# Hymba encoder trunk, first part of the projection: where ScalarE squares the weight chunks and who issues their loads

## Chip, cores and metric

One core of a Trainium2 chip runs the whole program in one launch. The metric is the device time of one execution in microseconds (us), median of several.

## What is computed

The reference is a hybrid encoder trunk of one layer on two groups of tokens (2048 and 256, model width 1024): a Hyena mixer and latent attention side by side, then an expert-choice mixture of experts. Only the start of it matters here, the normalisation and the input projection:

```python
def rms_norm(x, g):
    xf = x.astype(jnp.float32)
    y = xf * lax.rsqrt(jnp.mean(xf * xf, axis=-1, keepdims=True) + EPS)
    return (y * g.astype(jnp.float32)).astype(x.dtype)
...
u = rms_norm(x, attn_norm[l]) @ w_in[l]
y_h = hyena_mixer(u[..., :COL_HYENA], ...)
y_a = mla_mixer(u[..., COL_HYENA:COL_Q], u[..., COL_Q:COL_KV], u[..., COL_KV:], ...)
```

`w_in` has 1536 columns for the Hyena mixer and 416 for the attention.

## The kernel before, in words

The function `project` is the first of the phases, and everything behind it (attention, Hyena, experts) waits for it. It has two parts.

**First part.** A loop over 18 tiles of 128 tokens, one step t per tile, written out by hand on every engine and tied together by semaphores. The tile is normalised, turned (128x128 transposes on PE), split into a high and a low float16 half (`xT`, `xL`), and multiplied by the 416 attention columns (24 matmuls). In the same steps the 1536 Hyena columns, in 12 chunks of 128, are loaded one after another into the single buffer `wch` (512 KB) and squared, so that their common scale is known before the second part. The squares are sums of each chunk; the products are not made here.

In step t each engine does this:

- ScalarE: `square_x(t+2)` (L445), `copy_xT(t+1)` in two halves (L452), `square_chunk(t-2)` for 2 <= t < 14 (L481), `copy_c(t)` (L458, L462, L465), then it issues the load of chunk t-1 into `wch` on its own DMA queue (L517, the helper is L315). The load of chunk 0 is issued at the start (L491); the load that step 13 issues is chunk 0 again, for the second part.
- GpSimd: `root_x(t)` (L400, L402), the reciprocal root of the row's mean square.
- VectorE: `norm(t+2)` (L765), `copy_xT(t+1)`, the low halves (L770), and in some steps the filter angles (`angles` L778, `fold` L790), the scaling of small weights and of the norm gains.
- TensorE: `turn_x(t+1)` (L633), `make_c(t)` (L644), in step 5 also `hidden(1)` (L658).
- Sync engine: for t from 3 on it waits for `norm(t-3)` (the semaphore `normed`) and issues the rows of tile t (`copy_rows`, L170: four DMAs of 128 KB, one of 512 KB for the last two tiles). In its iteration t = 12 it also stores the size `S` (L353, 512 bytes), waits for the second sine (L354) and stores the filter's hidden values `H` (L356, two of 288 KB). Behind the loop it stores `VS` (L358, 512 bytes).

`make_c(t)` waits until `copy_c(t-1)` has emptied the PSUM bank (L639) and for the low halves of tile t (L637). `copy_xT(t+1)` waits for `turn_x(t+1)`; `turn_x(t+1)` waits for `norm(t+1)`.

**Second part.** 60 products of the split chunks with all tokens. Its first product waits for the last `copy_c` (L732) and for the split of chunk 0. The sync engine loads the chunks of this part (L362).

The wait and issue on ScalarE in the code:

```python
def square_chunk(n):
    act.wait_ge(wch_in, 16 * (n + 1))
    if n >= 2:
        act.wait_ge(w_squared["u"], n - 1)
    act.activation(wH[n % 2][:, :, :], wch[:, :, :], ACT.Square, scale=1 / MOST, accum_out=w_sum["u"][:, n:n + 1]
                   ).then_inc(w_squared["u"], 1)
```

Of the kernel before, what the change touches and what calls it, by code (L numbers as in the profile page):

```python
# [127 lines left out]
def rows(t, n=P):  # L128
    return bass.ds(t * n, n)
# [27 lines left out]
def tile_rows(ap, i):  # L157

    g = int(i >= NTP)
    J = P // (GROUPS[g] // N2)  # L160
    return ap.rearrange("(t i j) c -> i j t c", i=N2 // J, j=J)[i - g * NTP]


def copy_rows(eng, tile, ap, i, sem, store=False):
    g = int(i >= NTP)
    here = tile_rows(ap, i)
    n = 1 if g else P // (GROUPS[0] // N2)
    for m in range(n):
        part, whole = (tile, here) if g else (tile[m * P // n:(m + 1) * P // n, :], here[m])
        eng.dma_start(*((whole, part) if store else (part, whole))).then_inc(sem, 16)  # L170
# [14 lines left out]
def project(nc, io):  # L185
# [6 lines left out]
    NCH = CH // P  # L192
# [10 lines left out]
    with ExitStack() as ctx:  # L203
# [40 lines left out]
        def view(region, at, shape):  # L244
# [43 lines left out]
        w_squared, w_summed, w_sized, w_scaled, w_multiplied, w_backed = (  # L288
            {g: sem(f"{g}_{n}") for g in "cu"} for n in ("squared_w", "summed_w", "sized_w", "scaled_w", "multiplied", "backed"))
# [21 lines left out]
        def x_rows(t):  # L311
            return io["x_sample"][0] if t >= NTP else io["x_prompt"][0]

        def load_chunk(eng, n):
            eng.dma_start(wch[:, :, :], io["w_in"][0, :, n * P:(n + 1) * P].rearrange("(k p) f -> p k f", p=P)  # L315
                          ).then_inc(wch_in, 16)

        def part_of(w, i):
            return w[:, i * KP:(i + 1) * KP, :]

        @block.sync
        def _(sp):
            copy_rows(sp, x[0], x_rows(0), 0, x_in[0])
            sp.dma_start(gainx, io["attn_norm"].to_broadcast([P, D])).then_inc(gain_in, 16)
            sp.dma_start(eye[:, :], io["tab_eye"]).then_inc(gain_in, 16)
            for i in range(C_PARTS):
                sp.dma_start(part_of(wc, i), io["w_in"][0, i * KP * P:(i + 1) * KP * P, CH:].rearrange("(k p) f -> p k f", p=P)
                             ).then_inc(wc_in[i], 16)
            copy_rows(sp, x[1], x_rows(1), 1, x_in[1])
            copy_rows(sp, x[2], x_rows(2), 2, x_in[2])  # L330
            sp.wait_ge(cleared, 2)
            for half in range(2):
                f, h = slice(half * FEAT, (half + 1) * FEAT), slice(half * FH, (half + 1) * FH)
                for dst, src in ((feats[f, :], io["tab_feats"][:, half * W:(half + 1) * W]), (w1[f, h], io["filt_w1"][0]),
                                 (w2[h, h], io["filt_w2"][0]), (b1[h, :], io["filt_b1"]), (b2[h, :], io["filt_b2"]),
                                 (fr[h, :], io["filt_freq"])):
                    sp.dma_start(dst, src).then_inc(f_in, 16)
            sp.dma_start(qan[:, :], io["q_a_norm"]).then_inc(lt_in, 16)
            sp.dma_start(kvan[:, :], io["kv_a_norm"]).then_inc(lt_in, 16)
            sp.dma_start(gain[:, 0, :], io["q_norm"].to_broadcast([P, QH])).then_inc(lt_in, 16)  # L340
            sp.dma_start(gain[:, 1, :], io["k_norm"].to_broadcast([P, QH])).then_inc(lt_in, 16)
            sp.dma_start(wkv[:, :], io["w_ukv"][0]).then_inc(lt_in, 16)
            sp.dma_start(wq[:, :, :], io["w_uq"][0].rearrange("(k p) f -> p k f", p=P)).then_inc(lt_in, 16)
            sp.dma_start(rope[:, :, :], io["tab_rope"].rearrange("(n p) c -> p n c", p=P)).then_inc(lt_in, 16)
            for m in range(3):
                sp.dma_start(taps[:, m, :], io["conv_w"][:, m * NCH:(m + 1) * NCH]).then_inc(taps_in, 16)
            sp.dma_start(cbias[:, :], io["conv_b"]).then_inc(taps_in, 16)
            for t in range(XB, NT):
                sp.wait_ge(normed, t - XB + 1)
                copy_rows(sp, x[t % XB], x_rows(t), t, x_in[t % XB])  # L350
                if t == 12:
                    sp.wait_ge(sized, 6)
                    sp.dma_start(io["S"], size_in[:, 0:1]).then_inc(sized_out, 16)  # L353
                    sp.wait_ge(sines, 2)  # L354
                    for half in range(2):
                        sp.dma_start(io["H"][:, half * W:(half + 1) * W], h2[half * FH:(half + 1) * FH, :]).then_inc(h_stored, 16)  # L356
            sp.wait_ge(v_scaled, 2)
            sp.dma_start(io["VS"], v_back[:, :]).then_inc(sized_out, 16)  # L358
            for n in range(NCH + 2):
                if n + 1 < NCH:  # L360
                    sp.wait_ge(wL_made, n + 1)
                    load_chunk(sp, n + 1)  # L362
                if n >= 2:
                    sp.wait_ge(z_moved, NB * (n - 2) + 5)
                    sp.dma_start(io["Z"][NTP:, :, (n - 2) * P:(n - 1) * P].rearrange("i p c -> p i c"), zst[:, NTP:, :]
                                 ).then_inc(z_out[1], 16)
                if 1 <= n <= NCH:
                    sp.wait_ge(z_moved, NB * (n - 1) + 4)
                    sp.dma_start(io["Z"][0:NTP, :, (n - 1) * P:n * P].rearrange("i p c -> p i c"), zst[:, 0:NTP, :]
                                 ).then_inc(z_out[0], 16)  # L370
            sp.wait_ge(sized_out, 32)
            sp.wait_ge(h_stored, 32)
            for g in range(2):
                sp.wait_ge(z_out[g], 16 * NCH)
# [65 lines left out]
        def _(act):  # L440
            def square_x(t):
                act.wait_ge(x_in[t % XB], 16 * row_copies(t, XB))
                if t:
                    act.wait_ge(squared, t)
                act.activation(sqx, x[t % XB], ACT.Square, scale=D ** -0.5, accum_out=ms[:, t:t + 1]).then_inc(squared, 1)  # L445

            def copy_xT(t):
                act.wait_ge(x_turned, t + 1)
                if t == 0:
                    act.wait_ge(x_sized, 3)  # L450
                for k in (slice(0, KD // 2), slice(KD // 2, KD)):
                    act.activation(xT[:, k, rows(t)], pX[t % 2][:, k, :], ACT.Copy, scale=x_scale[:, 0:1]).then_inc(x_first, 1)  # L452

            def copy_c(t):
                act.wait_ge(c_made, t + 1)
                if t == 0:
                    act.wait_ge(w_backed["c"], 1)
                act.activation(c[:, t, :], pC, ACT.Copy, scale=w_back["c"][:, 0:1]).then_inc(c_moved, 1)  # L458
                act.wait_ge(c_moved, t + 1)
                if t:  # L460
                    act.wait_ge(c_squared, 2 * t)
                act.activation(junk[:, :], c[:, t, 0:QL], ACT.Square, scale=QL ** -0.5,  # L462
                               accum_out=msc[:, t, 0:1]).then_inc(c_squared, 1)
                act.wait_ge(c_squared, 2 * t + 1)
                act.activation(junk[:, 0:KVL], c[:, t, QL:QL + KVL], ACT.Square, scale=KVL ** -0.5,  # L465
                               accum_out=msc[:, t, 1:2]).then_inc(c_squared, 1)
# [5 lines left out]
            def move_size(g):  # L472
                act.wait_ge(w_summed[g], 1)
                act.activation(w_each[g][:, :], pW[g], ACT.Copy, accum_out=w_size[g][:, 0:1]).then_inc(w_sized[g], 1)
# [32 lines left out]
            for t in range(NT):  # L507
                if t + 2 < NT:
                    square_x(t + 2)
                if t + 1 < NT:  # L510
                    copy_xT(t + 1)
                if 2 <= t < NCH + 2:
                    square_chunk(t - 2)
                copy_c(t)
                if 2 <= t < NCH + 2:
                    act.wait_ge(w_squared["u"], t - 1)
                    load_chunk(act, (t - 1) % NCH)  # L517
                if t == NCH + 2:
                    move_size("u")
                if t == NCH + 3:  # L520
                    split_chunk(0)
                if t in (3, 9):
                    sine(t // 6)
                if t == 5:
                    act.wait_ge(scaled, 3)
                    act.activation(v_junk[:, :, :], w_of_v, ACT.Square, accum_out=v_sq[:, 0:1]).then_inc(v_squared, 1)
# [2312 lines left out]
```

## Time and profile before

| what | us |
|---|---|
| median of 3 runs | 3113.63 (3113.03 to 3119.89) |
| the profiled execution, its own time | 3118.16 |
| span of its trace | 3116.3 |
| PE / DVE / ACT / POOL busy | 2687.8 / 1809.8 / 1622.6 / 1049.9 |
| first product of the second part starts at | 155.84 |
| granted TensorE clock, mean | 0.936 of full speed |

The span is the trace's own length; the execution's time is 1.9 us longer. The first part takes the first 156 us of 3116, so no share of the whole says much of it: it has to be read from its own stretch.

### The profile page before, as it was taken

The page shows a single profiled execution, that of the slowest core. Times are in us where ns is not written, and L with a number is a line of the kernel's source. Part 1 is how long each engine was busy: PE and PEld are TensorE (multiplying, and loading weights), DVE is VectorE, ACT ScalarE, POOL GpSimd, SP SyncE. Part 2 cuts the span into 40 slices and gives each one's busy share as a digit, 9 for nine tenths or more (in the row PEclk, how much of TensorE's full clock was granted, in tenths as well). Part 3 has the DMA queues.
Part 4 walks back from the last instruction along what each step waited for, and adds up shares of the span by engine and source line. Part 5 has one row for each costly group of instructions (what it writes and reads, how often), then busy time and mean ns, then how long its engine had stood idle before and what let it go on. Part 6 is the DMA issues. An engine that isn't in the chain of part 4 may idle for free. (4 is left out here: it accounts for less than half of the span.)

```text
span 3116.3 us, 43460 instructions
## 1 busy us (share of the span) xinstructions
PE 2687.8 (86%) x15963; PEld 1475.5 (47%) x15963; DVE 1809.8 (58%) x2642; ACT 1622.6 (52%) x2560; POOL 1049.9 (34%) x976
## 2 busy tenths in 40 slices
PE   6799999689999999788968895999910799999998
PEld 4455555345555555432312232454510566666665
DVE  5455655378888888674567453333269455554552
ACT  6534444269999999774417442222240345544450
POOL 1121212168888888670037001111120112222221
PEclk9899999889999999999979997999955899999999
DMA  7423333424111111178957895443250466667662
GB/s 188 97 57 85 98 85 89 110 89 156 35 35 35 35 35 35 40 290 298 320 194 288 304 322 183 135 123 122 88 193 0 125 203 209 218 220 222 207 183 31
DMA packets 258673, 450.71 MB, mean 145 GB/s; under 512 B 55262, under 2 KB 148574, under 8 KB 256800
## 3 DMA queue, kind: packets, MB, share of 16 engines
q1 hardware_dynamic: 187616, 354.89, 34.6%
q10 hardware_dynamic: 60128, 55.73, 6.1%
q0 software_dynamic: 10752, 37.75, 5.3%
q8 instruction: 107, 1.75, 0.2%
q14 instruction: 70, 0.57, 0.1%
HBM read 296.55 MB, written 151.73 MB: 144 GB/s over the span
## 5 line engine op out<-in xcount | busy, mean ns | idle before, releaser
L1089 POOL TENSOR_TENSOR at_p<-at_pf,at_p 128x512 f16<-128x512 f32 x424 | 510.8, 1214 | 136.1 <-ACT at_p L1223 109.1
L1351 DVE TENSOR_REDUCE at_mxs<-at_pM 128x1 f32<-128x512 f32 x512 | 342.3, 685 | 72.6 <-PE at_pM L1250 61.6
L1222 ACT ACTIVATE at_pf<-at_pS,at_scale 128x512 f32<-128x512 f32 x520 | 358.3, 689 | 28.5 <-PE at_pS L1275 27.6
L1223 ACT ACTIVATE at_p<-at_pS,at_scale 128x512 f16<-128x512 f32 x520 | 355.3, 683 | 0.0
L1294 PEld LDWEIGHTS at_pO<-at_vv,at_p 128*128 128x128 f16 x4160 | 233.6, 97 | 140.3 <-POOL at_p L1089 31.9
L1294 PE MATMUL at_pO<-at_vv,at_p 128*128 128x129 f16 x4160 | 267.5, 207 | 8.3 <-POOL at_p L1089 6.5
L2108 PE MATMUL mg_pU<-z,mg_yT 128*128 128x512 f32 x576 | 252.3, 596 | 0.2 <-ACT mg_yT L2017 0.2
L2691 PE MATMUL ex_pY<-mo_down,ex_hT 128*128 128x512 f32 x512 | 224.0, 596 | 0.0
L1250 PE MATMUL at_pM<-at_k,at_q 96*128 96x512 f16 x512 | 189.5, 389 | 27.9 <-DVE at_q L1337 17.4
L1273 PE MATMUL at_pS<-at_q,at_k 97*128 97x512 f16 (+1 forms) x528 | 199.8, 378 | 3.9 <-issue 2.2
L1769 DVE TENSOR_TENSOR sp_pk<-sp_kk,sp_pX 128x512 f32<-128x512 f32 x152 | 104.5, 688 | 164.4 <-ACT sp_kk L1710 85.0
L1274 PE MATMUL at_pS<-at_q,at_k 96*128 96x512 f16 (+1 forms) x528 | 199.6, 378 | 0.0
L1275 PE MATMUL at_pS<-at_q,at_k 96*128 96x512 f16 (+1 forms) x528 | 198.4, 376 | 0.0
L2568 POOL TENSOR_TENSOR ex_mark<-ex_mark 128x1 f32<-128x1 f32 x64 | 12.0, 188 | 489.2 <-DVE ex_ys L2763 304.1
L2108 PEld LDWEIGHTS mg_pU<-z,mg_yT 128*128 128x128 f32 x576 | 108.3, 191 | 143.5 <-issue 140.3
L686 PE MATMUL pj_ps<-pj_xT,pj_wH 128*128 128x512 f16 (+1 forms) x480 | 171.9, 358 | 0.7 <-issue 0.7
L686 PE MATMUL pj_ps<-pj_xT,pj_wL 128*128 128x512 f16 (+1 forms) x480 | 171.8, 358 | 0.0
L686 PE MATMUL pj_ps<-pj_xL,pj_wH 128*128 128x512 f16 (+1 forms) x480 | 171.8, 358 | 0.0
L2691 PEld LDWEIGHTS ex_pY<-mo_down,ex_hT 128*128 128x128 f32 x512 | 96.1, 190 | 128.1 <-issue 128.1
L2741 DVE SCALAR_TENSOR_TENSOR ex_hT<-ex_pU,ex_back,ex_si 128x288 f32<-128x288 f32 x64 | 33.1, 518 | 203.5 <-PE ex_pU L2667 192.9
L1749 PE MATMUL sp_pG<-sp_pk,sp_tab 128*128 128x512 f32 x304 | 145.4, 600 | 5.5 <-DVE sp_pk L1769 5.4
L2667 PE MATMUL ex_pG<-ex_xT,mo_hi 128*128 128x288 f16 x512 | 147.2, 288 | 1.7 <-DVE ex_xL L2720 1.7
(306 smaller groups left out, 5726.9 us busy)
## 6 DMA issues: line engine op xcount, KB each, us to landing
sp_rows<-s_F SPq DMA_DIRECT2D x76, 768.0 KB, 6.9
s_F<-fs_a SPq DMA_DIRECT2D x72, 768.0 KB, 4.8
mo_raw<-in_w_gate SPq DMA_DIRECT2D x32, 1024.0 KB, 7.4
mo_raw<-in_w_up SPq DMA_DIRECT2D x32, 1024.0 KB, 7.6
mo_down<-in_w_down SPq DMA_DIRECT2D x16, 2048.0 KB, 10.1
s_G<-sp_gg ACTq DMA_DIRECT2D x72, 256.0 KB, 5.3
sp_tab<-tab_spec SPq DMA_DIRECT2D x76, 192.0 KB, 4.4
s_QK<-pj_R ACTq DMA_DIRECT2D x18, 768.0 KB, 4.7
```

What stands on the lines that cost most here:

```text
L686: last = pe.matmul(pU[n % 2][:, 0:width], w[ch % 2][:, k, :], x[:, k, t0:t0 + width], start=(k == 0 and w is wH and x is xT), stop=(k == K ...
L1089: eng.tensor_tensor(p2[r][:, :], pf[:, r, :], p1[r][:, :], ALU.subtract).then_inc(own_done if n in own else others_done, 1)
L1222: act.activation(pf[:, n % 4, :], pS[n % 2][:, 0:QB], ACT.Exp, scale=scale[:, 0:1])
L1223: act.activation(p1[n % 4][:, :], pS[n % 2][:, 0:QB], ACT.Exp, scale=scale[:, 0:1]).then_inc(pS_free, 1)
L1250: pe.matmul(pM[j % 2][:, :], q1[b][0:QH, tile * P:(tile + 1) * P], k1[b][0:QH, at:at + CW], start=True, stop=True).then_inc(slot_made, 1)
L1273: pe.matmul(out, k1[b][:, keys], q1[b][:, queries], start=True, stop=False)
L1274: pe.matmul(out, k1[b][0:QH, keys], q2[b][:, queries], start=False, stop=False)
L1275: last = pe.matmul(out, k2[b][:, keys], q1[b][0:QH, queries], start=False, stop=True)
L1294: last = pe.matmul(pO[qb % 2][:, t // 2, (t % 2) * VC:(t % 2) * VC + cols], part[r][:, t * P:(t + 1) * P], vv[b][:, of_v, 0:cols], start=( ...
L1351: dve.tensor_reduce(mxs[:, j // NC, j % NC:j % NC + 1], pM[j % 2][:, :], AX.X, ALU.max).then_inc(pM_free, 1)
L2108: last = pe.matmul(pU[:, h * 512:(h + 1) * 512], yT[t % 2][:, k, :], w[k][h], start=(k == 0), stop=(k == KD - 1))
L2691: last = pe.matmul(pY[0:n, h * 512:(h + 1) * 512], hT[:, f, starts[c]:starts[c] + n], wd[b][:, f, h * 512:(h + 1) * 512], start=(f == 0), ...
```

## The change

In ScalarE's step the square of the chunk moves behind `copy_c(t)`, and the wait and the load that ScalarE issued are gone. The sync engine issues these loads: in its iteration t >= 6, behind the rows of tile t, it waits until chunk t-6 is squared and loads chunk t-5 (chunk 0 again for t = 17). The load of chunk 0 at the start stays on ScalarE's queue.

```diff
@@ -348,6 +348,10 @@
             for t in range(XB, NT):
                 sp.wait_ge(normed, t - XB + 1)
                 copy_rows(sp, x[t % XB], x_rows(t), t, x_in[t % XB])
+                if t >= 6:
+
+                    sp.wait_ge(w_squared["u"], t - 5)
+                    load_chunk(sp, (t - 5) % NCH)
                 if t == 12:
                     sp.wait_ge(sized, 6)
                     sp.dma_start(io["S"], size_in[:, 0:1]).then_inc(sized_out, 16)
@@ -509,12 +513,9 @@
                     square_x(t + 2)
                 if t + 1 < NT:
                     copy_xT(t + 1)
+                copy_c(t)
                 if 2 <= t < NCH + 2:
                     square_chunk(t - 2)
-                copy_c(t)
-                if 2 <= t < NCH + 2:
-                    act.wait_ge(w_squared["u"], t - 1)
-                    load_chunk(act, (t - 1) % NCH)
                 if t == NCH + 2:
                     move_size("u")
                 if t == NCH + 3:
```

## Rows read from the trace of the kernel before

**Rows 1.** The page's first line

```profile
span 3116.3 us, 43460 instructions
```

**Rows 2.** Who waited for whom, 0 to 420 us: total, times, longest

```profile
ACT pj_wH L481 <- DMA pj_wch<-in_w_in: 29.3, 10, 7.5
```

**Rows 3.** ScalarE by time: start, duration, what it did, [idle before, releaser]

```profile
31.43 1.06 ACT L445 ACTIVATE pj_R<-pj_R 128x1024 bf16<-128x1024 f32 x1 [2.53 <-DMA pj_R<-in_x_prompt]
...
34.35 0.61 ACT L458 ACTIVATE pj_c<-pj_ps,pj_small 128x416 f32<-128x416 f32 x1 [0.62 <-PE pj_ps L644]
...
35.84 1.04 ACT L445 ACTIVATE pj_R<-pj_R 128x1024 bf16<-128x1024 f32 x1
...
40.59 0.61 ACT L458 ACTIVATE pj_c<-pj_ps,pj_small 128x416 f32<-128x416 f32 x1 [1.43 <-PE pj_ps L644]
...
41.78 0.43 ACTq L315 DMA_DIRECT2D pj_wch<-in_w_in  x1
...
42.31 1.06 ACT L445 ACTIVATE pj_R<-pj_R 128x1024 bf16<-128x1024 f32 x1
...
47.39 1.06 ACT L481 ACTIVATE pj_wH<-pj_wch 128x1024 f16<-128x1024 f32 x1 [2.78 <-DMA pj_wch<-in_w_in]
...
87.11 1.06 ACT L481 ACTIVATE pj_wH<-pj_wch 128x1024 f16<-128x1024 f32 x1 [6.70 <-DMA pj_wch<-in_w_in]
...
111.61 1.06 ACT L481 ACTIVATE pj_wH<-pj_wch 128x1024 f16<-128x1024 f32 x1 [4.53 <-DMA pj_wch<-in_w_in]
...
130.82 1.06 ACT L481 ACTIVATE pj_wH<-pj_wch 128x1024 f16<-128x1024 f32 x1 [7.53 <-DMA pj_wch<-in_w_in]
...
139.17 0.61 ACT L458 ACTIVATE pj_c<-pj_ps,pj_small 128x416 f32<-128x416 f32 x1 [3.35 <-PE pj_ps L644]
```

**Rows 4.** TensorE by time, the same columns

```profile
42.02 0.53 PE L644 MATMUL pj_ps<-pj_R,pj_xT 128*128 128x416 f16 x2 [0.23 <-DVE pj_xL L770]
...
46.07 0.34 PE L644 MATMUL pj_ps<-pj_R,pj_xL 128*128 128x416 f16 x1
...
61.34 2.10 PE L658 MATMUL pj_ps<-pj_R,pj_cn 128*128 128x512 f32 x6
...
88.89 0.85 PE L644 MATMUL pj_ps<-pj_R,pj_xT 128*128 128x416 f16 x2 [5.88 <-ACT pj_c L458]
...
155.84 0.38 PE L686 MATMUL pj_ps<-pj_xT,pj_wH 128*128 128x512 f16 x1 [0.74 <-issue]
```

**Rows 5.** Stretches of core 0: busy time by engine, then clock, DMA share, GB/s

```profile
88.00:94.00 6.00, 5.11 (x19) 2.39 (x20) 2.22 (x5) 4.89 (x12) 1.24 (x3) 0.62 0.31 87
...
101.00:112.00 11.00, 6.58 (x40) 3.98 (x40) 4.07 (x6) 4.80 (x12) 3.97 (x3) 1.00 1.00 242
```

**Rows 6.** The sync engine by time

```profile
76.99 0.42 SPq L353 DMA_DIRECT2D s_S<-pj_size_in  x1
97.93 1.12 SPq L356 DMA_DIRECT2D s_H<-pj_R  x2
99.09 7.09 SPq L170 DMA_DIRECT2D pj_R<-in_x_prompt  x12
...
119.47 0.35 SPq L358 DMA_DIRECT2D s_VS<-pj_v_back  x1
```

**Rows 7.** The tile `size_in`: landing of the store of `S`

```profile
DMA to landing us min/median/max: 7.8/7.8/7.8
```

**Rows 8.** VectorE by time

```profile
33.50 1.28 DVE L765 SCALAR_TENSOR_TENSOR pj_R<-pj_R,pj_rstd 128x1024 f32<-128x1024 f32 x1 [5.82 <-POOL pj_rstd L402]
34.70 1.40 DVE L770 SCALAR_TENSOR_TENSOR pj_xL<-pj_ps,pj_small,pj_xT 128x512 f16<-128x512 f32 x2
...
83.10 4.13 DVE L790 SCALAR_TENSOR_TENSOR pj_R<-pj_R 128x1152 f32<-128x1152 f32 x3
```

**Rows 9.** The tile `wch`, 0 to 140 us: landing of ScalarE's loads

```profile
DMA to landing us min/median/max: 3.7/4.5/10.3
```

**Rows 10.** The loads of `wch` that SyncE issues, second part

```profile
DMA to landing us min/median/max: 3.7/8.1/11.6
```

## The prediction

> **What bounds the kernel here.** The span is 3116.3 us [rows 1]; the change lies in its first 156 us, so I read that stretch alone. First the waits, for who is late: ScalarE stood idle before its square of a chunk 10 times, 29.3 us in all, each time for the chunk's load [rows 2]. Then ScalarE's own timeline, for why. Chunk 1's load was issued at 41.78, behind `copy_c`, and landed when the square started at 47.39, 5.6 us later. Between the two ScalarE had one square of x and one copy of xT to do, some 2.6 us of work, so 2.78 us were left over. The worst three waits were 6.70, 4.53 and 7.53 us [rows 3]. Then TensorE, for whether this matters: at 88.89 it had waited 5.88 us for `copy_c`, which stands behind the late square on ScalarE [rows 4], and its granted clock over 88 to 94 us was 0.62, so part of that step ran at 1.2 instead of 2.4 GHz [rows 5]. The second part's first product started at 155.84, where the first part ended [rows 4]. So the wait for a chunk is on the path that sets the end.
>
> From `copy_c(2)` at 40.59 to `copy_c(14)` at 139.17 the kernel took 98.6 us for 12 steps, 8.2 each [rows 3]. This is what the change can shorten. Steps 15 to 17 have no chunk and stay.
>
> The big waits have a cause of their own. The store of `S` was issued at 76.99, that of `VS` at 119.47 [rows 6]; each moves 4 bytes to a partition, and that of `S` took 7.8 us to land [rows 7]. The chunk loads issued right behind them are those of the squares at 87.11 and 130.82. The third, the square at 111.61, came behind the stores of `H` at 97.93 and twelve pieces of x rows at 99.09 [rows 6], with the DMA engines busy at share 1.00 and 242 GB/s [rows 5].
>
> **The change part by part.**
>
> *The issue leaves ScalarE.* From `copy_c` to the next square of x it took 1.72 us with the issue (40.59 to 42.31) and 1.49 without (34.35 to 35.84) [rows 3]: 0.23 us a step less. On SyncE the issue costs no engine anything while its queue isn't late.
>
> *The load gets a whole step.* It is issued when chunk n is squared and wanted when `copy_c` of the next step is done: a step less 1.05 us, 4.8 us if the step is 5.85 (below). Landing costs 3.7 us at best and 4.5 in the median [rows 9], with 0.3 taken as an estimate for SyncE to see the semaphore and issue (its wait is not in the trace of before; between nothing and the 0.43 of the issue row in [rows 3]). So 4.0 to 4.8 us, hidden. Upper end: the 5.6 of chunk 1, whose load ran beside x rows.
>
> *The square moves behind `copy_c`.* Before, without a late load, it filled time in which ScalarE waited for the matmuls anyway. Now it delays the next `square_x`, and through it a loop over two steps: from the end of `make_c(t-1)`, `copy_c` 1.5, square 1.05, then `square_x` to the start of `norm` 2.07 (31.43 to 33.50), `norm` to its successor 1.20, the low halves 1.40 [rows 3, 8], some 0.1 of hand-over, `make_c(t+1)` 4.39 (42.02 to 46.41) [rows 4]: 11.7 us for two steps, 5.85 each. Without the moved square the same loop is 5.3. So the move costs 0.5 a step against an ideal that the kernel of before never reached: it took 8.2.
>
> *What x rows pay.* SyncE now waits for squares ahead of them. Rows of tile t+1 go out behind chunk t-5, at the end of ScalarE's step t-4, and are wanted at the start of step t-1: two steps, 11.7 us. Free.
>
> *The small stores.* `S` now goes out behind chunk 7's load and `VS` behind the last load of chunk 0, so neither stands in front of a load that is wanted soon. The next load behind `S` is a step later.
>
> *The stores of `H`.* They still wait for the second sine. Then come the rows of tile 13 and only then chunk 8. From the times of before, x rows start 1.16 us behind `H` and four of twelve pieces take 2.4 us, so chunk 8 is issued 3.5 us behind `H`, with 0.58 + 0.52 + 0.52 = 1.62 MB on the queue: at 242 GB/s [rows 5] 6.7 us, plus some 1.6 of start-up (an estimate: 3.7 of [rows 9] less 0.52 MB at that rate), so it lands 8.3 us behind `H`. It is wanted 5.2 us behind `H`: a wait of some 3 us. From both sides: 0, and 6.7 (the first long wait of before).
>
> Here the order of queues weighs against the change. The wait of before at 111.61 had 12 pieces of x on SyncE's queue beside it, and the load on ScalarE's queue still got through 8.8 us after its issue. The Trainium skill, page "DMA: Bandwidth & Descriptors", section "Queues, rings and completion order", says that each DMA engine takes turns between the queues that have work: on ScalarE's own queue chunk 8 would get every other turn, on SyncE's it stands behind all of `H` and x. By that rule the load would be there about 2 us sooner on the old queue, and the forecast 2 us lower for a version that kept it there; the sum here already has it last in line.
>
> *The other engines' extra work.* VectorE's fold of the angles (4.13 us [rows 8], twice) and the six matmuls of `hidden(1)` (2.1 us [rows 4]) stay. Step by step, the fold in step 2 keeps `make_c(4)` where it was (+1.7 over 5.85), step 4's scaling of weights adds 0.7, `hidden(1)` 1.2, the second fold with the sine 1.8, chunk 8 3.1, small differences the rest: 8.6 us.
>
> **Sum.** 12 x 5.85 + 8.6 = 78.8 us for the 12 steps, against 98.6: **19.7 us less** (`copy_c(14)` at 119.4 instead of 139.2). This holds TensorE at full clock in the stretch. The later phases are unchanged and start that much sooner. The profiled execution of 3118.2 would become 3098.5; it stands 4.5 above the median, and the median of 3113.6 becomes 3093.9. I say 3094.
>
> **The rivals.**
>
> *Loads at 5.6 us (chance 0.15).* The chunk's load and the x rows issued right behind it share the engines in every step. The square then waits for its load: a step is 1.05 + 0.3 + 5.6 = 6.95. In some 7 steps that nothing else lengthens this adds 1.1: 8 us. For it: chunk 1 did so beside x rows [rows 3]. Against it: those x rows had been issued ahead of the load, now they go out behind it. Time 3102.
>
> *The small store clogs again (0.12).* `S` is issued 0.4 us behind chunk 7's load. If it slows a load that is still on its way, this one lands after some 10 us as before and not after 4: 5.5 us given back. Time 3099.5. The Trainium skill, page "DMA: Bandwidth & Descriptors", "Specifications", has transfers under 512 bytes done as read-modify-write. It names no price, and whether that can slow a load already on its way no run here shows.
>
> *Nothing gained (0.06).* Another gate opens the second part: the split of chunk 0 or the conditions before `products`. Against it: its first matmul came 0.7 us after the start of the last `copy_c`. Time 3113.
>
> *Slower (0.05).* SyncE's own loads of this tile in the second part took 8.1 us in the median [rows 10]. If a load on SyncE's queue costs that here too, because x rows of the step before are still ahead of it, the squares go by the load alone: 1.05 + 0.3 + 8.1 = 9.45 a step, from the first at 42.1 to the twelfth at 146.1, and `copy_c(14)` some 4.7 later, at 150.8: 11.6 us later than before, 3125. It decides from a mean landing of 7.05 us on, where `copy_c(14)` comes out at 139.2. Against it: in the second part the load stands beside stores of 1 MB, here beside 0.5 MB of x that has 5 us to drain.
>
> **How the numbers follow.** The forecast has 0.62. Its own range is 3089 (no wait for chunk 8, landings fully hidden, 24.7 less) to 3098 (the wait at its upper end). The range of 8 in 10 takes in the two rivals above it and stretches for mixed cases: 3088 to 3106. A measurement of this kernel can tell 0.2%, 6.2 us, from no change. Faster by more than that: the forecast and the first two rivals, 0.89, less 0.02 for a mixture that falls short: 0.87. Within: 0.08. Slower: 0.05.
>
> **What the profile of the changed kernel would show.** The group of ScalarE waiting at L481 for `wch` falls from 29.3 to 3 to 5 us, nearly all of it in chunk 8. `copy_c` starts every 5.6 to 6.2 us in undisturbed steps. In their place ScalarE waits at L458 for the matmuls. TensorE waits for `copy_c` no longer than 3 us at a time and keeps its clock. The second part's first matmul starts near 136. Wrong if L481 still waits in most steps (landings above 4.8), if steps are over 6.5 us with no wait at L481 (the two-step loop is longer than I have it), or if the second part starts early and the end does not come earlier.

## The result and the profile after

| what | before | after |
|---|---|---|
| median, us | 3114.65 (3113.03 to 3119.89, 6 runs) | 3102.66 (3099.25 to 3106.16, 6 runs) |
| ratio after to before | | 0.9949, 95% interval 0.9935 to 0.9964 |
| span of the profiled execution | 3116.3 | 3097.4 |
| first product of the second part | 155.84 | 139.18 |
| `copy_c(2)` to `copy_c(14)` | 98.6 | 81.5 |

The kernel is 0.5% faster, 15.9 us by the ratio, with the interval from 11.2 to 20.2. The two medians in the table are only 12.0 us apart, which lies in that interval. Forecast were 19.7 less and 3094, with a range of 3088 to 3106. The direction and the range hold; the gain came out a fifth smaller by the ratio, and the median is 8.7 us above 3094.

The profile after: the page's first line, then who waited for whom from 27 to 140 us.

```profile
span 3097.4 us, 43460 instructions
```

```profile
ACT pj_c L462 <- PE pj_ps L645: 26.3, 17, 3.6
...
ACT pj_wH L485 <- DMA pj_wch<-in_w_in: 5.0, 3, 3.8
```

The wait for a chunk, 29.3 us in ten pieces [rows 2], is now 5.0 in three. ScalarE waits for the matmuls instead, as it should where TensorE is to set the pace. ScalarE by time, where the 5.0 us are and what they do (the columns are those of [rows 3]):

```profile
40.98 0.61 ACT L462 ACTIVATE pj_c<-pj_ps,pj_small 128x416 f32<-128x416 f32 x1 [1.82 <-PE pj_ps L645]
...
75.80 1.06 ACT L485 ACTIVATE pj_wH<-pj_wch 128x1024 f16<-128x1024 f32 x1 [0.76 <-DMA pj_wch<-in_w_in]
...
94.05 0.61 ACT L462 ACTIVATE pj_c<-pj_ps,pj_small 128x416 f32<-128x416 f32 x1 [1.66 <-PE pj_ps L645]
...
99.39 1.06 ACT L485 ACTIVATE pj_wH<-pj_wch 128x1024 f16<-128x1024 f32 x1 [3.75 <-DMA pj_wch<-in_w_in]
...
102.62 0.60 ACT L462 ACTIVATE pj_c<-pj_ps,pj_small 128x416 f32<-128x416 f32 x1
...
110.83 0.61 ACT L462 ACTIVATE pj_c<-pj_ps,pj_small 128x416 f32<-128x416 f32 x1 [2.78 <-PE pj_ps L645]
...
122.51 0.61 ACT L462 ACTIVATE pj_c<-pj_ps,pj_small 128x416 f32<-128x416 f32 x1 [1.70 <-PE pj_ps L645]
```

Chunk 8 is the late one. From `copy_c(10)` at 94.05 to `copy_c(12)` at 110.83 it is 16.8 us, 5.1 more than the 11.7 that the forecast gives to two steps, for a wait of 3.75. TensorE and its clock (third column from the right in the second view) show where the other 1.3 went:

```profile
103.84 1.97 PE L634 MATMUL pj_ps<-pj_eye,pj_R 128*128 128x128 f32 x8 [4.62 <-DVE pj_R L766]
...
110.63 1.04 PE L634 MATMUL pj_ps<-pj_eye,pj_R 128*128 128x128 f32 x8
...
139.18 0.38 PE L687 MATMUL pj_ps<-pj_xT,pj_wH 128*128 128x512 f16 x1 [0.74 <-issue]
```

```profile
103.00:107.00 4.00, 3.16 (x13) 2.32 (x14) 2.10 (x3) 3.42 (x10) 0.02 (x1) 0.60 0.71 181
```

TensorE stood idle 4.62 us, and over 103 to 107 us its granted clock was 0.60 of full speed, so part of that stretch ran at 1.2 GHz: eight transposes took 1.97 us, at full clock 1.04. In the kernel before it was the same behind the wait of 5.88 us, where the clock was 0.62 [rows 4, 5]. The sync engine, for the order of the DMAs:

```profile
82.52 0.39 SPq L315 DMA_DIRECT2D pj_wch<-in_w_in  x1
82.95 0.58 SPq L357 DMA_DIRECT2D s_S<-pj_size_in  x1
90.23 1.12 SPq L360 DMA_DIRECT2D s_H<-pj_R  x2
91.39 3.30 SPq L170 DMA_DIRECT2D pj_R<-in_x_prompt  x4
94.73 0.42 SPq L315 DMA_DIRECT2D pj_wch<-in_w_in  x1
...
118.65 0.38 SPq L315 DMA_DIRECT2D pj_wch<-in_w_in  x1
119.07 0.68 SPq L362 DMA_DIRECT2D s_VS<-pj_v_back  x1
```

Both small stores now go out 0.4 us behind a load; before, they were 0.6 and 1.1 us ahead of one. Chunk 8's load is issued at 94.73, 4.5 us behind `H`, because the four pieces of x ahead of it took 3.30 us to issue; it landed in 4.7.

### The profile page after: what moved, and what is told of

It is laid out like the page before. It is cut to its first block and busy times, and to the rows that moved or that the text cites. A ratio compares the mean times of both kernels' runs of the same rounds, so it can differ in the third digit from the quotient of the medians.

```text
span 3097.4 us, 43460 instructions
## 1 busy us (share of the span) xinstructions
PE 2682.7 (87%) x15963; PEld 1470.1 (47%) x15963; DVE 1810.5 (58%) x2642; ACT 1621.9 (52%) x2560; POOL 1054.9 (34%) x976
```

## The experiments

Every run below has its own number; the table lists them by what they change, not in the order in which they were made. The measure that tells them apart is the stretch from `copy_c(2)` to `copy_c(14)` in one profiled execution, since the rest of the program varies by more than most of these edits are worth: span less first product was 2956.1 to 2962.5 us in 13 of the 14 profiles, 2967.3 in one. "Waits" is ScalarE's idle time before the square for the chunk's load, with the longest.

| run | square | load issued by | stores | waits, us | stretch | first product | ratio, interval |
|---|---|---|---|---|---|---|---|
| before | first | ACT, last | early | 29.3 (7.5) | 98.6 | 155.8 | 1 |
| the change | last | SP | early | 5.0 (3.8) | 81.5 | 139.2 | 0.9949 (0.9935 to 0.9964) |
| e11, the change | last | SP | early | 11.6 (7.0) | 86.4 | 144.0 | 0.9956 (0.9940 to 0.9972) |
| e1 | last | ACT, last | early | 7.3 (3.9) | 85.0 | 144.6 | 0.9974 (0.9963 to 0.9984) |
| e2 | first | SP | early | 11.2 (8.9) | 80.9 | 138.8 | 0.9939 (0.9926 to 0.9953) |
| e3 | last | SP | `H` later | 3.5 (2.2) | 79.4 | 137.6 | 0.9932 (0.9918 to 0.9947) |
| e4 | last | SP | `S` ahead | 15.1 (7.2) | 90.5 | 148.1 | one execution |
| e5 | first | ACT, last | `S`, `VS` late | 16.2 (4.3) | 83.6 | 141.3 | 0.9944 (0.9928 to 0.9959) |
| e12 | last | SP | `S`, `VS` late | 5.9 (5.0) | 83.6 | 141.2 | 0.9947 (0.9935 to 0.9959) |
| e10 | last | SP, ahead of x | early | 5.8 (3.9) | 81.7 | 139.5 | 0.9945 (0.9930 to 0.9961) |
| e9 | first | ACT, last | all late | 14.4 (2.8) | 79.2 | 136.9 | 0.9946 (0.9931 to 0.9962) |
| e8 | first | ACT, early | all late | 7.7 (1.6) | 77.5 | 136.3 | 0.9924 (0.9909 to 0.9939) |
| e7 | last | SP | all late | 0.3 (0.3) | 76.0 | 134.1 | 0.9924 (0.9908 to 0.9939) |
| e6 | first | SP | all late | 0.4 (0.2) | 71.7 | 129.4 | 0.9921 (0.9907 to 0.9935) |

**e1, the order alone.** Of the change, only the square moved; ScalarE issues the load right behind it.

Against the kernel before:

```diff
                 if t + 1 < NT:
                     copy_xT(t + 1)
+                copy_c(t)
                 if 2 <= t < NCH + 2:
                     square_chunk(t - 2)
-                copy_c(t)
-                if 2 <= t < NCH + 2:
                     act.wait_ge(w_squared["u"], t - 1)
                     load_chunk(act, (t - 1) % NCH)
```

> Only the order changes: the square of the chunk stands behind copy_c, ScalarE still issues the next chunk's load, right behind the square. If what counts is that a load gets a whole step, this has it too. But the store of S and that of VS are then free again to go out just ahead of a chunk's load, since the sync engine no longer waits for squares. Theory (the small stores clog the loads behind them): two landings of about 10 us come back, less the 4.8 us that a step now hides: two waits of some 5 us, a third of some 4 behind the stores of H, 12 to 15 us of waiting at the square in all; copy_c(2) to copy_c(14) about 93 us, against 98.6 before and 81.5 with the whole change; the whole about 0.2% faster than before. Rival (only the longer cover counts, the queue does not matter): waits of 4 to 6 us in all, 82 to 84 us, 0.5% faster.

The waits came to 7.3 us and the stretch to 85.0, between the two and close to the rival's 82 to 84; the whole time, 0.26% less, is close to the theory's 0.2%. So the moved square alone shortens the stretch by 13.6 us. Of the two slow landings that were expected both came, but only one as a long wait. ScalarE by time (its DMA issue is ACTq), and the sync engine:

```profile
77.52 0.38 ACTq L315 DMA_DIRECT2D pj_wch<-in_w_in  x1
...
86.02 1.06 ACT L481 ACTIVATE pj_wH<-pj_wch 128x1024 f16<-128x1024 f32 x1 [3.09 <-DMA pj_wch<-in_w_in]
```

```profile
77.31 0.42 SPq L353 DMA_DIRECT2D s_S<-pj_size_in  x1
...
115.61 0.35 SPq L358 DMA_DIRECT2D s_VS<-pj_v_back  x1
```

Chunk 6's load, 0.2 us behind `S`, took 8.5 us to land. `VS` fell 0.3 us behind chunk 11's load (115.29), and this one took 7.5 (its square started at 122.75). I had counted on `VS` being ahead. Both slow landings have a small store beside them, and the longer cover hid most of each.

**e2, the queue alone.** The square is ahead of `copy_c` again. Against the changed kernel:

```diff
+                if 2 <= t < NCH + 2:
+                    square_chunk(t - 2)
                 copy_c(t)
-                if 2 <= t < NCH + 2:
-                    square_chunk(t - 2)
```

> Only the queue changes: the sync engine issues the loads, the square stands ahead of copy_c as before. The load is issued as soon as the chunk is squared, so it too gets a whole step. Theory (the moved square costs 0.5 us a step through the loop over two steps, the rest of the gain is the early issue and the small stores out of the way): as fast as the whole change or up to 3 us faster, copy_c(2) to copy_c(14) 78 to 82 us. Rival (the order is what gains, because a late chunk no longer holds copy_c): waits at the square hold copy_c and TensorE, 86 us or more, slower than the whole change by 4 us or more.

As forecast: 80.9, and that with a wait of 8.87 us at chunk 8, which in this order holds `copy_c`. The steps before and after were 5.2 to 5.5 us where nothing else was in them. So nothing of this gain needs the moved square: 17.7 us of the stretch come from the queue alone, and e1's 13.6 from the order alone are no gain on top of it, since the whole change brings 17.1.

**e3, the stores of `H` later.**

Against the changed kernel; the store of `S` stays at 12:

```diff
                     sp.wait_ge(sized, 6)
                     sp.dma_start(io["S"], size_in[:, 0:1]).then_inc(sized_out, 16)
+                if t == 15:
                     sp.wait_ge(sines, 2)
                     for half in range(2):
```

> The whole change, with the stores of H issued three iterations of the sync engine later (t = 15), where chunk 8 and the rows of tile 13 are long out. Theory (the wait for chunk 8, 3.75 us, and the half clock behind it come from H and x on the queue ahead of it): the wait at chunk 8 falls below 1 us, TensorE keeps its clock, copy_c(2) to copy_c(14) 76 us instead of 81.5. A smaller wait may come at chunk 10 or 11, up to 2 us, with 78. Rival (that wait is the rows of x alone): it stays at 3 us or more.

The wait at chunk 8 fell from 3.75 to 1.04 us, just above the expected 1, so most of it was `H`'s. But a wait of 2.23 came up at chunk 7, whose load had `S` 0.43 us behind it and landed after 7.6 us, and the stretch is 79.4 instead of 76.

**e4, the store of `S` 0.4 us ahead of chunk 7's load** instead of behind it. Against the changed kernel:

```diff
+                if t == 12:
+                    sp.wait_ge(sized, 6)
+                    sp.wait_ge(w_squared["u"], t - 5)
+                    sp.dma_start(io["S"], size_in[:, 0:1]).then_inc(sized_out, 16)
                 if t >= 6:
...
                 if t == 12:
-                    sp.wait_ge(sized, 6)
-                    sp.dma_start(io["S"], size_in[:, 0:1]).then_inc(sized_out, 16)
                     sp.wait_ge(sines, 2)
```

> The whole change, with the 512-byte store of S issued just ahead of chunk 7's load instead of just behind it. Theory (its 4-byte pieces clog what stands behind them for about 8 us): the square of chunk 7 waits 4 to 5 us for its load where the whole change has no wait, landing 9 to 10 us. Rival (the two long landings of before had another cause): landing of chunk 7 about 4 to 5 us, no wait.

The sync engine, and ScalarE:

```profile
82.87 0.35 SPq L354 DMA_DIRECT2D s_S<-pj_size_in  x1
83.27 0.43 SPq L315 DMA_DIRECT2D pj_wch<-in_w_in  x1
```

```profile
94.34 1.06 ACT L487 ACTIVATE pj_wH<-pj_wch 128x1024 f16<-128x1024 f32 x1 [6.65 <-DMA pj_wch<-in_w_in]
```

The load of 512 KB took 11.1 us behind 512 bytes, and the square waited 6.65 us; in the two profiles of the change it waited nothing and 3.79 (e11, below). The stretch grew by 9.0 us against the first of them and by 4.1 against the second. Part of this is chunk 8, which waited 7.22 us here, 3.75 and 7.01 there. It is one execution.

**e5, the kernel before with only `S` and `VS` moved** behind the twelfth square; nothing of the change. Against the kernel before:

```diff
                 if t == 12:
-                    sp.wait_ge(sized, 6)
-                    sp.dma_start(io["S"], size_in[:, 0:1]).then_inc(sized_out, 16)
                     sp.wait_ge(sines, 2)
...
+            sp.wait_ge(w_squared["u"], NCH)
+            sp.wait_ge(sized, 6)
+            sp.dma_start(io["S"], size_in[:, 0:1]).then_inc(sized_out, 16)
             sp.wait_ge(v_scaled, 2)
             sp.dma_start(io["VS"], v_back[:, :]).then_inc(sized_out, 16)
```

> The kernel before, with the stores of S and VS both behind the twelfth square, so that no chunk load stands behind them; the stores of H stay. Theory (4-byte pieces clog what is behind them): the waits of 6.70 and 7.53 us at the squares of chunks 6 and 11 fall to 1 to 1.5 each, as the undisturbed ones, the waits at the square sum to 17 to 18 us instead of 29.3, and copy_c(2) to copy_c(14) takes 85 to 87 us instead of 98.6: two thirds of what the whole change brought, without moving the square or the queue. Ratio to before about 0.996. Rival: the two waits stay, nothing changes.

ScalarE, the two squares that had waited 6.70 and 7.53 [rows 3]:

```profile
81.11 1.06 ACT L482 ACTIVATE pj_wH<-pj_wch 128x1024 f16<-128x1024 f32 x1 [1.11 <-DMA pj_wch<-in_w_in]
...
118.38 1.06 ACT L482 ACTIVATE pj_wH<-pj_wch 128x1024 f16<-128x1024 f32 x1 [1.11 <-DMA pj_wch<-in_w_in]
```

1.11 us each, as forecast; the stretch came to 83.6, below the 85 to 87 expected. It fell by 15.0 us, where the change brought 17.1, and the ratio is the change's own, within the intervals. So two stores of 512 bytes had cost nearly as much as the whole change gives back. The slow landing moved along with them: the load of chunk 0, issued 1.1 us behind `S` and 0.7 behind `VS`, landed after 11.4 us, where only the second part waits for it, 0.17 us long.

**e9, e8, e7, e6: what the two moves are worth with all stores out of the way.** `H`, `S` and `VS` go behind the loop in all four:

```diff
-                if t == 12:
...
+            sp.wait_ge(w_squared["u"], NCH)
+            sp.wait_ge(sines, 2)
+            for half in range(2):
+                sp.dma_start(io["H"][:, half * W:(half + 1) * W], h2[half * FH:(half + 1) * FH, :]).then_inc(h_stored, 16)
+            sp.wait_ge(sized, 6)
+            sp.dma_start(io["S"], size_in[:, 0:1]).then_inc(sized_out, 16)
             sp.wait_ge(v_scaled, 2)
```

e9 is the kernel before, e7 the change. e6 is e2's order with the sync engine's loads. e8 has ScalarE issue the load, between its square and `copy_c`:

```diff
                 if 2 <= t < NCH + 2:
                     square_chunk(t - 2)
-                copy_c(t)
-                if 2 <= t < NCH + 2:
                     act.wait_ge(w_squared["u"], t - 1)
                     load_chunk(act, (t - 1) % NCH)
+                copy_c(t)
```

> The kernel before with the stores of H, S and VS behind the loop, nothing of the change. Theory (29.3 us of waiting were half stores, half a load issued too late): the ten waits of 0.5 to 2.6 us stay, 11 to 13 us in all, no wait above 3; copy_c(2) to copy_c(14) 78 to 80 us, so the change's own two moves are worth only 2 to 4 us once the stores are out of the way; ratio near 0.994. Rival (with the stores gone the loads land within their cover): waits under 4 us, 72 us.

> The square ahead of copy_c as before, ScalarE issues the next load itself, but right behind the square and ahead of copy_c; the stores of H, S and VS behind the loop. Theory (what helps is the early issue, and the queue costs ScalarE only its 0.23 us for each load): 70 to 73 us from copy_c(2) to copy_c(14), 1 to 3 more than with the sync engine's issue; ratio about 0.991. Rival (on its own queue the load shares the engines with rows of x issued by the sync engine and lands in 5.6 us, later than a step gives it): waits of 1 us in most steps, 76 to 80 us.

> The whole change with the stores of H, S and VS behind the loop. It differs from the run with the square ahead of copy_c only in that order. Theory (the moved square lengthens a loop over two steps to 5.85 a step): copy_c(2) to copy_c(14) 74 to 76 us, 4 to 6 us more than with the square ahead; ratio to before about 0.992; two consecutive steps add up to 11.7 us where VectorE has nothing else. Rival (the order costs nothing): both alike within 1 us.

> The sync engine issues the loads (as in the change), the square stays ahead of copy_c (as before), and the stores of H, S and VS all go behind the loop. Theory: nothing long is left in front of a load, the step is that of TensorE, 5.2 to 5.4 us, waits at the square under 2 us in all; copy_c(2) to copy_c(14) 68 to 71 us, first product of the second part near 127; the fastest, ratio to before about 0.990. Rival (in this order every small delay of a load holds copy_c): 76 us or more.

e9: 79.2 as forecast, waits of 0.2 to 2.8 us, 14.4 in all where 11 to 13 were expected: with the stores gone, the change's two moves are worth 3.2 us (to e7's 76.0). e8: 77.5, the rival's number, with waits of 0.2 to 1.6 us in nine steps. The loads land later than in e6; the landing lines of the tile `wch`, 0 to 125 us, for e8 and then e6:

```profile
DMA to landing us min/median/max: 3.8/5.2/5.8
```

```profile
DMA to landing us min/median/max: 3.7/4.2/5.6
```

Two things differ between e8 and e6: the queue of the loads, and the times of the rows of x, which in e6 wait for squares and in e8 do not. Which of the two makes the loads later is not shown.

e7 against e6 is the order alone: 4.3 us, within the 4 to 6 expected. `copy_c` in e7, then e6:

```profile
94.02 0.61 ACT L462 ACTIVATE pj_c<-pj_ps,pj_small 128x416 f32<-128x416 f32 x1 [1.66 <-PE pj_ps L645]
99.23 0.61 ACT L462 ACTIVATE pj_c<-pj_ps,pj_small 128x416 f32<-128x416 f32 x1 [0.40 <-PE pj_ps L645]
105.70 0.61 ACT L462 ACTIVATE pj_c<-pj_ps,pj_small 128x416 f32<-128x416 f32 x1 [1.27 <-PE pj_ps L645]
111.30 0.61 ACT L462 ACTIVATE pj_c<-pj_ps,pj_small 128x416 f32<-128x416 f32 x1 [0.79 <-PE pj_ps L645]
117.38 0.61 ACT L462 ACTIVATE pj_c<-pj_ps,pj_small 128x416 f32<-128x416 f32 x1 [1.28 <-PE pj_ps L645]
```

```profile
96.67 0.61 ACT L462 ACTIVATE pj_c<-pj_ps,pj_small 128x416 f32<-128x416 f32 x1 [0.36 <-PE pj_ps L645]
...
102.13 0.61 ACT L462 ACTIVATE pj_c<-pj_ps,pj_small 128x416 f32<-128x416 f32 x1 [0.40 <-PE pj_ps L645]
...
107.30 0.61 ACT L462 ACTIVATE pj_c<-pj_ps,pj_small 128x416 f32<-128x416 f32 x1 [0.37 <-PE pj_ps L645]
112.77 0.61 ACT L462 ACTIVATE pj_c<-pj_ps,pj_small 128x416 f32<-128x416 f32 x1 [1.70 <-PE pj_ps L645]
```

In e7 two steps add up to 11.68 (94.02 to 105.70, 105.70 to 117.38), the loop of the forecast (11.7); in e6 they are 5.2 to 5.5 each. e6's stretch, 71.7, is just above the 68 to 71 expected. e6 is faster than before by 0.8% and, by the ratios, than the change by 0.3%. Its whole times do not set it apart from e7 and e8, though its second part starts 4.6 and 6.8 us earlier: the spread of the later phases covers that.

**e11, e10, e12: what delays the loads of chunks 7 and 8.** The three were made against the changed kernel. e11 is the change again. e10 puts the chunk's load ahead of the rows of x in each iteration, e12 puts `S` and `VS` behind the loop and leaves `H`. The edit of e10:

```diff
             for t in range(XB, NT):
+                if t >= 6:
+                    sp.wait_ge(w_squared["u"], t - 5)
+                    load_chunk(sp, (t - 5) % NCH)
                 sp.wait_ge(normed, t - XB + 1)
                 copy_rows(sp, x[t % XB], x_rows(t), t, x_in[t % XB])
-                if t >= 6:
-                    sp.wait_ge(w_squared["u"], t - 5)
-                    load_chunk(sp, (t - 5) % NCH)
```

> The changed kernel itself, beside the next two on one chip. If the spread of the comparisons lies in the later phases, its first part is as in its profile (first product at 139 us, within 1) and its ratio to before lies between 0.993 and 0.996.

> The whole change, but in each iteration the sync engine issues the chunk's load ahead of the rows of x, so chunk 8 stands behind the stores of H only, and the rows of tile 13 stand behind it. Theory (what is ahead on the queue delays chunk 8, in proportion to its bytes): its wait falls from 3.75 to about 1 us; the rows of tile 13 are then late instead, 1 to 2 us before square_x; copy_c(2) to copy_c(14) 79 to 81 us against 81.5. Rival (H itself is what is slow, x adds nothing): wait of 3 us or more.

> The whole change with the stores of S and VS behind the loop; the stores of H stay in iteration 12. Theory (the store of S, issued 0.4 us behind chunk 7's load, holds up that load's landing in about half of the executions, and H's own writes make chunk 8 late): no wait at chunk 7 in any profile, 3 to 5 us at chunk 8, copy_c(2) to copy_c(14) 79.5 to 82 us, first product 137 to 139.5; the six executions no longer fall into two groups, ratio 0.9935 to 0.9945. Rival (the store of S also slows H and chunk 8 behind it): the wait at chunk 8 under 1.5 us as well, 77 us.

e11 was a surprise: same kernel, first product at 144.0, 4.9 us later, outside what I expected. Chunk 7 waited 3.79 us, and chunk 8 7.01 instead of 3.75. The sync engine and ScalarE:

```profile
82.33 0.38 SPq L315 DMA_DIRECT2D pj_wch<-in_w_in  x1
82.76 0.58 SPq L357 DMA_DIRECT2D s_S<-pj_size_in  x1
```

```profile
91.44 1.06 ACT L485 ACTIVATE pj_wH<-pj_wch 128x1024 f16<-128x1024 f32 x1 [3.79 <-DMA pj_wch<-in_w_in]
```

And the DMA view of 85 to 88 us, 40 slices of 0.075 us, with the packets:

```profile
GB/s 341 369 362 335 288 254 173 51 21 20 20 20 1 0 0 0 0 0 0 0 0 0 0 0 0 0 0 0 0 0 0 0 0 0 0 0 0 0 0 0
DMA packets 489, 0.17 MB, mean 56 GB/s; under 512 B 160, under 2 KB 489, under 8 KB 489
```

The last packets moved by 86.0, and the square was let go at 91.44. It is the completion that came 5.4 us late, not the data. So the rival "the small store clogs again" fits some executions and not others. In five profiles a small store follows a load of a chunk that is squared next within 0.45 us: three of these loads landed late (7.5, 7.6, 9.1 us), two did not (4.4, and 5.4 in the first profile of the change). Where no small store followed so soon, chunk 7's load landed after 3.9 (e12), 4.3 (e10) and 4.6 us (e7). But the last load of chunk 0 has such a store 0.4 us behind it in six profiles (the change, e11, e2, e3, e4, e12), and it landed after 3.8 to 5.0 us in all of them. So three late landings in eleven pairs: that the store is the cause is likely and not proved, and what else it takes is open.

The whole times fit two groups: of the change's twelve executions five lie at 3099.3 to 3101.1 and seven at 3104.4 to 3107.7; the profile without the wait is of the first group, that with it of the second. In e12, without the store there, the six lie within 3100.0 to 3103.3. Two groups in twelve executions, two of them profiled, are a reading and not a proof. Against it speaks that the six of e10, where the store of `S` stands behind the rows of x, 2.4 us after chunk 7's load, spread over 9.9 us, and that e12's ratio, 0.9947, is no better than the change's own.

e10: the wait at chunk 8 stayed at 3.86 us although the rows of x stood behind it now. The rival's number came: what is slow is mainly standing behind `H`. The load was issued 1.2 us behind `H` and landed at 99.34, 9.3 us behind it; in the change, issued 4.5 us behind, it landed at 99.39, 9.2 us behind `H`. Against that one profile, half a megabyte of x less ahead of it made no difference. But with x between, the other profiles have the landing 10.4 (e12), 10.6 (e11), 10.9 (e4) and 11.0 us (e2) behind `H`, and in e10 the stores of `H` themselves landed after 5.4 to 5.9 us instead of 3.3 to 4.1. So x may add up to 1.8 us; one profile of each does not settle it. The rows of x were expected 1 to 2 us late behind chunk 8; ScalarE waited 0.16 us for them there. e12: 4.99 us at chunk 8, no wait at chunk 7; a wait for chunk 8 is there without the store of `S`. The stretch, 83.6, missed the expected 82 at most: behind that wait TensorE stood for 5.9 us, and the eight transposes that followed took 1.97 us again, against 1.04 at full clock.

## Why the prediction came out as it did

**What bounds, right.** The wait for a chunk is on the path, and the later phases start sooner by what the first part loses: first product 16.7 us earlier, span 18.9 shorter. That the profiled execution came out at 3099.3 where 3098.5 was forecast is in part luck: its first product is 3.1 us later than forecast, and the phases behind it happened to be 2.2 us shorter than in the profile before.

**Where the gain comes from, right in its parts, wrong in its weights.** The text treated the small stores as one cause beside the late issue. Against a kernel that has them in front of its loads, each of three edits alone gives most of the gain of 17.1 us in the stretch: the stores moved 15.0 (e5), the queue 17.7 (e2), the order 13.6 (e1). The three do not add up, because each of them keeps the two slow landings off the path or hides them in part. With the stores out of the way, the change's own two moves are worth 3.2 us (e9 to e7).

**The issue leaves ScalarE, the load gets a whole step: right.** Landings of 3.7 to 5.6 us, hidden but for 0.76 and 0.52 us at two chunks.

**The moved square costs 0.5 a step: right where nothing else is in the step.** Two steps are 11.68 us, 5.84 each, in e7 and 5.2 to 5.5 each in e6. Over all twelve steps it is 4.3 us, 0.36 a step, since steps that something else lengthens pay less. Once the sync engine issues the loads, it is a loss: with the square left where it was, the stretch is 0.7 us shorter in spite of a wait of 8.87 us (e2), and 4.3 shorter without the stores.

**The rest of the sum: right.** Without chunk 8's 3.1 us it gives 75.7, and e7, where no load is late, took 76.0. Two slips are in the numbers: 98.6 less 78.8 is 19.8, not 19.7, and the lower end of the range, 24.7 less, cannot come from the sum, where only the 3.1 of chunk 8 can be saved (22.9 less, 3091).

**The small stores are harmless behind a load: wrong in some executions.** This term stood at nothing in the sum and was given as a rival with 0.12 and a price of 5.5. In e11 chunk 7 waited 3.79 us, and the first product came at 144.0: 4.9 us later than in the other profile of the change, 2.9 later than in e12, which has no such store there. How much of the 4.9 is the store's is open, since chunk 8 waited longer too. In the first part the forecast was 19.7 less; one profile of the change has the first product 16.7 us earlier, the other 11.8, and the ratio's 15.9 lies between them.

**Chunk 8, the right place, too small.** This is the term that was mis-sized in both profiles. I put the wait at 3.1 and took all of it as the step's loss, from bytes over bandwidth. It was 3.75, 4.99 and 7.01 us in three profiles of this order (the change, e12, e11), and cost more than itself: 5.1 us for 3.75, because TensorE stood 4.62 us and then ran in part at 1.2 GHz (0.60 of full speed over 103 to 107 us). The forecast had TensorE keep its clock and wait 3 us at most. I had 8.3 us from `H` to the landing; it was 9.2 to 11.0. `H` makes most of that (e3); how much the rows of x add is open, at most 1.8 us (e10). The Trainium skill, page "DMA: Bandwidth & Descriptors", section "Queues, rings and completion order", has each DMA engine take turns between the queues that have work, from which the prediction took some 2 us less for a load kept on ScalarE's queue. e1 keeps it there: chunk 9's load, issued 6.3 us behind `H` beside twelve pieces of x, landed after 8.4 us, and its square waited 3.94. No gain of 2 us shows, but the load is another one, and so this is no clean test of the rule.

**"Nothing gained" and "slower"** did not occur. "Loads at 5.6 us" did not either: its 3102 is next to the measured median, but in the change the median landing was 4.3 us, so this is a coincidence. That is also far from the mean of 7.05 us from which the loads would have set the pace.

## What to carry to other kernels

Look at what was issued just ahead of the slowest landings before moving any load: here a store of 4 bytes to a partition held up a load of 512 KB behind it by 4 to 7 us, and moving two such stores was worth nearly the whole change. Do not add up what several edits gain alone: they may all cure the same two waits. Fill the time in which an engine waits for TensorE anyway: work that stands behind the wait instead of in it lengthens the loop between engines. And when the same kernel's profile differs by 5 us from one execution to the next, take a second profile before you weigh the terms.

## What the runs showed of the hardware that was not expected

Five loads of 512 KB were issued 0.2 to 1.1 us behind a store of 512 bytes, on its queue or on the other one. They landed after 9.5 and 10.3 us (before), 8.5 (e1), 11.1 (e4) and 11.4 (e5), where the median of these loads was 4.5 us in the kernel before [rows 9].

A small store 0.3 to 0.45 us behind a load went with a late completion in three of eleven cases. In e11 the load's completion came 5.4 us after its data had moved. The Trainium skill, page "DMA: Bandwidth & Descriptors", section "Queues, rings and completion order", has the completion land only after the earlier writes of the same DMA engine. Here the small writes were issued later. Whether they are what holds it, and by what way, stays open.

Behind the two stores of `H`, 288 KB each, a load of 512 KB issued 1.2 us later landed after 8.1 us (e10).
